# A two-block transformer step on one core: the opening cut into chunks of x, small loads on other queues, the ending token tile by token tile

## What is computed

```python
def rms_norm(x, g):
    y = x * rsqrt(mean(x * x, -1) + EPS)
    return y * g

z = rms_norm(x, mix_norm_g) @ w_in        # mLSTM heads, their gates (mi, mf), attention heads, gate ff
...                                       # mLSTM, forgetting attention, w_out, conv FFN, gated embedding
...                                       # second block: relative attention, pooling, mixing
x = x + swiglu(rms_norm(x, norm_ffn), w_gate_up, w_down)
return rms_norm(x, norm_final)
```

## Time and profile before

| what | value |
|---|---|
| median of 3 runs | 2632.29 us (2632.16 to 2632.94) |
| profiled execution | 2631.81 us |
| its span | 2630.2 us |
| PE busy | 2603.1 us, 99% |
| DVE, ACT, POOL busy | 1421.8, 1211.2, 99.5 us |
| DMA, mean rate | 183 GB/s |
| granted clock, mean | 0.998 |

### The profile page before, as it was taken

The page is one execution under the profiler, slowest core; times in us unless marked ns, Lnnn a source line. Parts: engine busy times, 40 slices in busy tenths (PEclk is TensorE's granted clock), DMA queues, the critical chain, the costliest instruction groups (busy, mean ns, idle before and its releaser), DMA issues.

```text
span 2630.2 us, 35295 instructions
## 1 busy us (share of the span) xinstructions
PE 2603.1 (99%) x12070; PEld 2174.2 (83%) x12070; DVE 1421.8 (54%) x1687; ACT 1211.2 (46%) x1502; POOL 99.5 (4%) x151
## 2 busy tenths in 40 slices
PE   8999999999999999999999999999999999999998
PEld 6889998888888888888887888888888888888886
DVE  5555655666666664445656555555545454454444
ACT  4444544545445444444554444444544444443443
POOL 1000220000000000002001100000000000000000
PEclk9999999999999999999999999999999999999999
DMA  5655655666666665666665656665666666666664
GB/s 174 181 169 147 164 169 184 184 185 185 187 183 185 183 189 192 191 190 189 201 181 165 179 167 191 189 190 189 186 192 183 192 191 187 190 189 196 204 192 144
DMA packets 358993, 481.99 MB, mean 183 GB/s; under 512 B 22798, under 2 KB 170560, under 8 KB 358784
## 3 DMA queue, kind: packets, MB, share of 16 engines
q1 hardware_dynamic: 353376, 476.27, 60.7%
q0 software_dynamic: 1232, 3.45, 0.6%
q10 hardware_dynamic: 4304, 1.19, 0.2%
HBM read 478.71 MB, written 2.12 MB: 183 GB/s over the span
## 4 chain that ended last, share of the span: by engine, by line
PE 86%; issue 11%; POOL 1%; DVE 1%; ACT 0%; ACTq 0%; POOLq 0%
PE acc L1384 28%; PE acc L1386 28%; PE acc L1385 27%; PE T L1399 1%; PE T L1603 1%; POOL fsq_s L1821 0%; POOL small L1823 0%; PE X L1613 0%; PE X L1718 0%; POOL fqk_s L1826 0%; DVE small L1027 0%; PE T L1698 0%; PE X L1708 0%; ACTq L510 0%; ACT xt_hi L503 0%
## 5 line engine op out<-in xcount | busy, mean ns | idle before, releaser
L835 DVE TENSOR_TENSOR wlo<-raw,whi 128x1024 fp32r<-128x1024 f32 (+1 forms) x916 | 1102.7, 1207 | 988.3 <-ACT whi L485 987.4
L485 ACT ACTIVATE whi<-raw 128x1024 fp32r<-128x1024 f32 (+1 forms) x916 | 950.4, 1044 | 1100.9 <-PE acc L1386 1094.5
L1384 PE MATMUL acc<-whi,xt_hi 128*128 128x512 f32 (+1 forms) x2176 | 842.4, 387 | 3.2 <-DVE wlo L835 3.2
L1386 PE MATMUL acc<-whi,xt_lo 128*128 128x512 f32 (+1 forms) x2176 | 834.9, 384 | 0.0
L1385 PE MATMUL acc<-wlo,xt_hi 128*128 128x512 f32 (+1 forms) x2176 | 834.3, 383 | 0.0
L1384 PEld LDWEIGHTS acc<-whi,xt_hi 128*128 128x128 f32 x2176 | 409.4, 188 | 79.4 <-issue 5.9
L1386 PEld LDWEIGHTS acc<-whi,xt_lo 128*128 128x128 f32 x2176 | 408.9, 188 | 75.2
L1385 PEld LDWEIGHTS acc<-wlo,xt_hi 128*128 128x128 f32 x2176 | 409.4, 188 | 73.4
L1384 PE MATMUL acc<-whi,ht_hi 128*128 128x512 f32 x704 | 274.7, 390 | 0.0
L1386 PE MATMUL acc<-whi,ht_lo 128*128 128x512 f32 x704 | 274.3, 390 | 0.0
L1385 PE MATMUL acc<-wlo,ht_hi 128*128 128x512 f32 x704 | 274.2, 389 | 0.0
(11 more groups left out here) (269 smaller groups left out, 1506.8 us busy)
## 6 DMA issues: line engine op xcount, KB each, us to landing
raw<-in_w_up_dram SPq DMA_DIRECT2D x176, 512.0 KB, 3.6
raw<-in_w_down_dram SPq DMA_DIRECT2D x176, 512.0 KB, 4.6
raw<-in_w_gate_up_dram SPq DMA_DIRECT2D x176, 512.0 KB, 4.3
raw<-in_w_in_dram SPq DMA_DIRECT2D x256, 256.0 KB, 3.2
raw<-in_w_out_dram SPq DMA_DIRECT2D x64, 512.0 KB, 4.5
raw<-in_w_in_dram SPq DMA_DIRECT2D x64, 512.0 KB, 3.7
raw<-in_w_in_dram SPq DMA_DIRECT2D x128, 192.0 KB, 2.9
raw<-in_w_ple_gate_dram SPq DMA_DIRECT2D x32, 512.0 KB, 4.3
```

Source lines behind the costliest of these rows:

```text
L485: act.activation(whi[:, s, :, 0:w.width], raw[:, s, :, 0:w.width], ACT.Copy).then_inc(hi_made, 1)
L835: dve.tensor_tensor(wlo[:, s, :, 0:w.width], raw[:, s, :, 0:w.width], whi[:, s, :, 0:w.width].bitcast(F32), ALU.subtract).then_inc(lo_made, 1)
L1384: pe.matmul(out_, h_, wh_, start=(j == 0 and kk == 0), stop=False)
L1386: done = pe.matmul(out_, l_, wh_, start=False, stop=(j == w.n - 1 and kk == KS - 1))
```

## The change

**Order of loads.** SP issues x chunk 0, stages 0 and 1, chunk 1, stages 2 and 3, chunks 2 and 3. The 14 parameter loads go to POOL, behind its constants. The gate columns are loaded in 8 pieces of 512 runs, two for each quarter of the rows, from ACT, behind its stages 2, 3, 4 and 5.

**Opening by half chunks.** Chunks use two pairs of banks in turn (T1, T2 and `acc[1]`). ACT and DVE split half a chunk at a time and put the halves between their first stages; PE transposes chunk 1 behind stage 0, chunk 2 behind 2, chunk 3 behind 3. PE also does 14 matmuls of ones whose result nobody reads (`awake`): 6 at once, 2 behind the gain's transpose, 6 behind chunk 0. ACT does one small copy at the start. The gate products move from ahead of stage 6 to ahead of stage 7, `gates_turn` to behind 7, and `rows_turn`, `cols_turn`, `m_scores` each one stage later; so do DVE's steps of the gates.

**Ending.** In the last window PE does stages 0 to 17 as before, then the last four stages for tile 0 and then for tile 1. Add, squares, mean, 1/rms, scaling and 4 stores of 256 KB follow for each tile on its own; the last column block is scaled by 1/rms and gain in one operation.

```diff
-            for n in range(NB):
+            def x_load(n):
                 sp.dma_start(xres[:, :, n * W:(n + 1) * W], ...).then_inc(x_landed[n], 16)
...
-            mlstm_loads(0, {SLOTS - 1: [load_parameters]})
+            x_load(0)
+            mlstm_loads(0, {1: [lambda: x_load(1)], 3: [lambda: x_load(2), lambda: x_load(3)]})
...
+            for t in range(T):
+                sp.wait_ge(out_left[t], 1)
+                store(t, 0, W)
+                sp.wait_ge(out_made[t], 1)
+                store(t, W, 2 * W)
...
 # ACT
-            act.dma_start(wg_raw[:, :, 0:2 * MH], w_in_k[:, :, 4 * MW:FOX0])...
-            act.dma_start(wg_raw[:, :, 2 * MH:NG], w_in_k[:, :, FOX0 + 3 * FH * FD:])...
+            act.wait_ge(ones_set, 1)
+            act.activation(sq_out[:, 0:1], ones[:, 0:1], ACT.Copy)
...
-            for n in range(NB):
-                split("init", n, xt_hi, g_mix)
-            mlstm(0, True, {1: [gate_w_split], 3: [first_square(0), first_square(1)], 4: [first_square(2), first_square(3)]},
-                  {0: [logits_exp], 1: [gains_copy]}, [em_exp])
+            start_half(0, 0)
+            mlstm(0, True, {0: [lambda: start_half(0, 1)], 2: [*start_both(1), lambda: gate_weights(0)],
+                            3: [first_square(0), lambda: gate_weights(1)], 4: [*start_both(2), lambda: gate_weights(2)],
+                            5: [*start_both(3), lambda: gate_weights(3)], 6: [first_square(1), gate_w_split],
+                            7: [first_square(2), first_square(3)]},
+                  {1: [logits_exp], 2: [gains_copy]}, [em_exp])
...
 # DVE
+            start_half(0, 0)
+            mlstm(0, True, {0: [lambda: start_half(0, 1)], 2: start_both(1), 4: start_both(2), 5: start_both(3),
+                            6: [gate_w_split], 7: [gate_copy]})
...
 # PE
+            pe.wait_ge(ones_set, 1)
+            awake(6)
+            pe.wait_ge(const_made, 1)
             pe.wait_ge(mix_gain_landed, 16)
             pe.transpose(bank[X1][:, 0:KD], gain_rows[0:KD, :], ident[0:KD, 0:KD]).then_inc(mix_gain_turned, 1)
+            awake(2)
+            start_turn(0)
+            awake(6)
...
+                    before = {j: [start_ready(j)] for j in range(2 * NB)}
+                    before[7].append(gate_products)
+                    after_a = {0: [lambda: start_turn(1)], 2: [lambda: start_turn(2)], 3: [lambda: start_turn(3)],
+                               7: [gates_turn, gains_turn]}
+                    after_b = {2: after_b[2], 3: [rows_turn], 5: [cols_turn], 6: after_b[4]}
...
+            def multiply_last(w, high, low):
...
+                for t in range(T):
+                    for j in range(w.n - SLOTS, w.n):
+                        pe.wait_ge(lo_made, w.stages_to(j))
+                        done = products(acc[w.par][t][:], w, high, low, j, t, False, j == w.n - 1)
...
+                    if t == 0:
+                        done.then_inc(first_ended, 1)
```

More of the change, by code:

```diff
@@ L992, in m_split, with mlstm @@
                 done.then_inc(bank_read[T2], 1)
-            def mlstm(h, first):
+            def mlstm(h, first, early={}):
                 a, b = pair_windows("mlstm", h)
@@ L1011, in mlstm, with start_half, start_both @@
                 lo(b, after_b)
-            for n in range(NB):
-                split("init", n, xt_hi, xt_lo, g_mix)
-            mlstm(0, True)
+            def start_half(n, half_):
+                dve.wait_ge(split_hi, 4 * n + 2 * half_ + 2)
+                for kk in range(2):
+                    k = 4 * n + 2 * half_ + kk
+                    done = dve.scalar_tensor_tensor(xt_lo[:, k, :], start_bank[n % 2][half_][:, kk * S:(kk + 1) * S],
+                                                    gains[:, g_mix + k:g_mix + k + 1], xt_hi[:, k, :].bitcast(F32),
+                                                    ALU.mult, ALU.subtract)
+                done.then_inc(start_split, 1)
+            def start_both(n):
+                return [lambda: start_half(n, 0), lambda: start_half(n, 1)]
+            start_half(0, 0)
+            mlstm(0, True, {0: [lambda: start_half(0, 1)], 2: start_both(1), 4: start_both(2), 5: start_both(3),
+                            6: [gate_w_split], 7: [gate_copy]})
             with dve.Fori(1, MH) as h:
@@ L1353, in _ @@
                 lo(ws[n], {3: [lambda: add(n - 1, ws[n - 1])], 8: [lambda: squared_times_gain(n - 1)]})
[L1354 to L1363, removed]
+            norm, w = NORM["down2"], ws[-1]
+            last = slice((NB - 1) * W, NB * W)
+            for t in range(T):
+                if t == 0:
+                    dve.wait_ge(first_ended, 1)
+                else:
+                    dve.wait_ge(stage_used, w.end())
+                dve.tensor_tensor(xres[:, t, last], acc[w.par][t][:], xres[:, t, last], ALU.add).then_inc(last_added, 1)
+                dve.wait_ge(square_done, T * (NB * norm + NB - 1) + t + 1)
+                dve.tensor_reduce(meansq[:, norm, t:t + 1], sumsq[:, norm, t, :], AX.X, ALU.add).then_inc(last_mean, 1)
+                dve.wait_ge(last_rstd, t + 1)
+                dve.wait_ge(gained, T * (NB - 1))
+                for n in (1, 2):
+                    x = xres[:, t, n * W:(n + 1) * W]
+                    dve.tensor_scalar(x, x, rstd[:, norm, t:t + 1], None, ALU.mult).then_inc(out_made[t], 1)
+                dve.scalar_tensor_tensor(xres[:, t, last], xres[:, t, last], rstd[:, norm, t:t + 1], gfin[:, last],
+                                         ALU.mult, ALU.mult).then_inc(out_made[t], 1)
         @block.tensor
@@ L1638, in hidden_then_down, with products @@
                         after = {**after, **extra}
-                    multiply(ws[n], ht_hi, ht_lo, after=after)
+                    if down == "down2" and n == NB - 1:
+                        multiply_last(ws[n], ht_hi, ht_lo)
+                    else:
+                        multiply(ws[n], ht_hi, ht_lo, after=after)
                 return ws[-1]
+            def products(out_, w, high, low, j, t, start, stop):
+                s = w.slot(j)
+                for kk in range(KS):
+                    k = KS * j + kk
+                    h_, l_ = high[:, k, t * P:(t + 1) * P], low[:, k, t * P:(t + 1) * P]
+                    pe.matmul(out_, h_, whi[:, s, kk, :], start=start and kk == 0, stop=False)
+                    pe.matmul(out_, h_, wlo[:, s, kk, :], start=False, stop=False)
+                    done = pe.matmul(out_, l_, whi[:, s, kk, :], start=False, stop=stop and kk == KS - 1)
+                return done
+            def multiply_last(w, high, low):
+                reached(pe, acc_read[w.par], 2 * w.block)
+                for j in range(w.n - SLOTS):
+                    pe.wait_ge(lo_made, w.stages_to(j))
+                    for t in range(T):
+                        done = products(acc[w.par][t][:], w, high, low, j, t, j == 0, False)
+                    done.then_inc(stage_used, 1)
+                for t in range(T):
+                    for j in range(w.n - SLOTS, w.n):
+                        pe.wait_ge(lo_made, w.stages_to(j))
+                        done = products(acc[w.par][t][:], w, high, low, j, t, False, j == w.n - 1)
+                        if t == T - 1:
+                            done.then_inc(stage_used, 1)
+                    if t == 0:
+                        done.then_inc(first_ended, 1)
             def p_turn():
@@ L1887, in _ @@
             norm(NORM["out2"])
-            norm(NORM["down2"])
+            n = NORM["down2"]
+            for t in range(T):
+                pool.wait_ge(last_mean, t + 1)
+                pool.tensor_scalar(meansq[:, n, t:t + 1], meansq[:, n, t:t + 1], 1.0 / D, EPS, ALU.mult, ALU.add).then_inc(last_eps, 1)
+                pool.wait_ge(last_eps, t + 1)
+                pool.tensor_tensor(rstd[:, n, t:t + 1], meansq[:, n, t:t + 1], half[:, 0:1], ALU.pow).then_inc(last_rstd, 1)
 _INS = ["x", "p", "mix_norm_g", "w_in", "mlstm_gate_bias", "mlstm_out_g", "fox_q_g", "fox_k_g", "fox_f_bias", "w_out",
```

127 lines of the change are left out of this document (77 added, 50 removed).

## The result

The changed kernel takes **2618.32 us** (median of 5 runs, 2617.97 to 2618.39), the kernel before, run beside it on the same chip, 2632.40 (5 runs, 2632.16 to 2632.94). The ratio is 0.9945, its 95% interval 0.9934 to 0.9956: 14.1 us less, where 12.0 were forecast. The profiled execution took 2617.97 us, its span is 2616.3, against 2631.81 before.

The account below looks back on a forecast made before the run. PE, busy for 99% of the span, was taken as the bound except in the opening and ending. Gains of 8.3 us and 3.7 us, together 12.0, taken from 2632.29 gave 2620.3 us, range 2617.0 to 2626.0.

Parts of the forecast that it names:

- One of its own signs of being wrong: ACT's queue in the opening: the forecast is wrong if gate issues exceed 1.5 us a pair.
- Start of stage 0: Opening: PE's first stage matmul starts at 9.5 us instead of 21.05, bounds 9.0 and 10.0.
- The clock: Opening: idle matmuls keep PE's clock at the upper level from stage 0 on, saving 1.3 us.
- Rival (a): Opening: the clock stays low, idle matmuls not being enough or PE cooling before stage 0; 2622 us, chance 0.12.
- Transposes of three chunks: Opening: 3 x 8 transposes now fall between PE's stages and add 3.0 us.
- The wait at stage 6: Opening: ACT's queue, with 5.0 us for four gate pairs, makes PE wait 0.8 us for stage 6's weights.
- Rival (d): ACT's queue: every gate issue costs like L510's 4.49 us, a price per issue; +27 us, 2647 us, chance 0.05.
- rival (b): Opening: ACT is the bound, its reserve used up by gate pairs or late gate columns; 2623.5 us, chance 0.12.
- The wait at `m_turn`: Opening: the log sigmoid's chain, one stage later, makes PE wait 0.8 us, bounds 0 and 2.
- Sum of the opening: From the start to the mark: 69.0 us against 77.29, 8.3 us gained.
- Parameters and stage 4's loads: Opening: 14 parameter loads on POOL and stage 4's loads issued behind all of x cost nothing.
- The ending: Last matmul to the end: 8.5 us instead of 12.2, 3.7 us gained, bounds 3.0 and 4.2.

Follow-up runs that it names:

- the repetition: The changed kernel, unaltered, run once more in the last set of runs: 2618.23 us.
- Experiment 8: Changed kernel with all four chunks of x transposed and split ahead of stage 0, load order left as it is: 2629.16 us.
- experiment 3: Changed kernel without its 14 idle matmuls of ones: 2620.44 us.
- Experiments 6: Changed kernel with the gate loads as two large ones at the front of ACT's queue, as before the change: 2619.34 us.
- experiment 7: Changed kernel with all eight gate loads issued in a row behind stage 2: 2623.75 us.
- experiment 5: Changed kernel with the 14 parameter loads back on SP, behind the loads of x: 2618.66 us.
- experiment 1: Kernel before the change, with the change's ending and the old opening: 2628.92 us, ratio 0.9985.
- experiment 2: Kernel before the change, with the change's opening and the old ending: 2621.78 us, ratio 0.9958.
- experiment 4: Changed kernel without its last 6 idle matmuls, those between chunk 0's transposes and stage 0: 2620.10 us.
- experiment 9: Changed kernel with chunk 0 loaded in halves, the last six idle calls split, and each tile's first block stored by ACT: 2618.03 us.
- 10: Changed kernel with stage 0's weights loaded ahead of x and `whi` made before chunk 0 is split: 2620.08 us.

## Why the prediction was right, and where its sum was not

The forecast's mechanism held: 2620.3 forecast, 2618.3 measured, PE's own work between the first stage and the last matmul, and the gain at its two ends. The terms of its sum were off by up to 0.8 us each, most to the same side. One of its own signs of being wrong did appear, a pair of gate issues of more than 1.5 us (19.70 and 20.11, 0.37 + 1.76), and it cost PE nothing.

- **Start of stage 0.** 9.5 forecast, 9.47 in the trace, in the order that was worked out: transposes, `xt_hi` at 6.28, `whi` at 7.01, `wlo` at 8.10. In the repetition the weights were the last to land, and it was 9.77, within the bounds given. Experiment 8 shows that with these loads it takes the interleaving; what the freed front would give without it is not shown.
- **The clock.** Stage 0 runs at 0.23 at once, worth 1.7 us by experiment 3 (1.3 in the sum). The Trainium skill (TensorE: Matmul & The Clock Gate, What's actually happening) says that the clock is throttled by default and that activity releases the throttle. Experiment 3 agrees, 2.1 us slower without matmuls of ones, whose result nobody reads. Rival (a) was real as a mechanism, and the idle matmuls keep it off.
- **Transposes of three chunks.** 3.0 us forecast, 0.8 each measured, 2.4: the 1.04 us of the row includes the last one's tail, over which the next matmul starts.
- **The wait at stage 6**, 0.8 us forecast, none seen: the mis-sized term. The step "per run that makes 1.24 us for a pair" took 4.49 us, a row in which the queue was occupied by the load ahead of it, and spread them over runs, all of it on ACT's path: 5.0 us for the four pairs. The eight issues of the changed kernel take 4.87 us together, seven of them 0.37 to 0.55 each beside activations or a wait for data; only the one of 1.76 held ACT, for 1.14 us. So `wlo` of stage 6 was made at 27.0 and not at 29.5, and PE came to it at 28.6: 1.6 us of slack in place of a wait of 0.8. By the page DMA: Bandwidth & Descriptors of the Trainium skill (Issuing engines are not separate DMA queues) the time to initiate a DMA is usually small relative to the DMA itself; for seven of the eight issues the trace sides with that. Experiments 6 and 7 side with the row of L510: 3.8 us, and 1.25 to 1.53 us for issues in close order. Rival (d), a price per issue whatever the distance, falls; rival (b) has its mechanism shown by experiment 7, in another order of the issues.
- **The wait at `m_turn`**, 0.8 forecast with a lower bound of 0, none seen. The loss of slack was right (0.07 us are left of 2.4), but that no wait came of it is as much luck as reckoning: DVE reached `qk_s` at 47.72, where about 50 was forecast, and had it written at 48.46; PE wanted it at 48.53, where about 49 was forecast.
- **Sum of the opening**: 8.3 forecast, 10.1 measured. The three terms above make 2.2 of that difference of 1.8; most of the remaining 0.4 the other way stands in PE's rows. The first matmul of stage 0 and the first behind each of the three chunks (9.47, 13.08, 19.41, 23.03) stand 0.31 to 0.32 ahead of the next and not 0.23, 0.3 us together, for which the sum had nothing.
- **Parameters and stage 4's loads**, costed at nothing: right. The loads on POOL took 0.5 us each (the first 0.73) and were out at 11.1, and experiment 5 shows that SP could have carried them too.
- **The ending**: 8.5 us forecast, 8.4 measured, 3.7 and 3.8 gained; experiment 1 by itself gives 3.9. The stores moved 371, 311 and 328 GB/s in the three microseconds of data, less than the 406 assumed, but they began a little earlier.

## What to carry to other kernels

When PE is busy for 99% of the span, look at what stands before its first and behind its last matmul: clear the queues that hold the first stage, interleave the preparation of the inputs with the first stages, and finish one output tile while the other is still being multiplied. Fill PE's gaps ahead of the first stage with idle matmuls, but retime them with every change of the loads, for where data comes late they stand in the way. Spread DMA issues of many small runs on a computing engine's queue out beside its activations, at most a pair at a time as here, never all in a row.

## What the hardware showed beyond the expectation

- **An issue on ACT's queue runs beside ACT's activations.** L532 at 13.37 and L533 at 13.80 lie inside the activations from 12.93 to 14.5. The price appears when many issues of small runs follow closely: 0.45, 0.57, 0.56, then 1.25, 1.53, 1.44 us in experiment 7, and everything behind them on ACT waits. Distance isn't all of it: the second issue of the third pair took 1.76 us in the change, 1.78 in the repetition, 1.28 in experiment 5, 1.02 in experiment 2, and 0.53 to 0.60 in experiments 3, 4, 9 and 10. Why is open.
- **The clock was down behind PE's gaps of 2.85 us and more, and still up behind those of 1.85 us and less.** PE idle ahead of the first slow matmul: 2.85 (experiment 4), 2.99 (6), 3.53 (7), each behind transposes or matmuls at the upper level (in experiment 4 it rose within the transposes, which took 1.42 us). Idle ahead of a fast one: 1.51 in the change's profile, 1.85 in that of its repetition, 1.64 in experiment 5. Between 1.85 and 2.85 no run has a gap with the upper level before it and work behind it. The length of the gap isn't all of it either: behind the last matmul of the program the granted clock fell some 4.1 us after PE's end in the change's profile and some 2.2 us after it in that of experiment 9, estimated from the means of 0.98 and 0.55 in the microseconds from 2611 and from 2610.
- **When the clock rises differs by execution.** The same first sixteen idle matmuls were followed by chunk 0's transposes in 1.09 us (the change), 1.60 (experiment 7) and 1.82 (experiment 8). It cost experiment 2 some 0.35 us at stage 0 (9.82).
- **Half a load moved its reader little.** In experiment 9, with half of chunk 0 to wait for, the transposes started 0.15 us earlier and `xt_hi` 0.02.
